# Sample rows in layer 1's paired products: the shared first product is made once and added twice, instead of being run into two accumulators

## What is computed

```python
def dil_layer(x, dil_fn, mem_kv, norm_g, w_in, q_norm_g, mem_q_g, w_out):
    z = rms_norm(x, norm_g) @ w_in                 # x: 2048 prompt rows, and 8 sample rows
    qd, gd, mq, mg = jnp.split(z, [...], axis=-1)
    ...
def shared_kv(x, kv_norm_g, w_kv, k_norm_g):
    kv = (rms_norm(x, kv_norm_g) @ w_kv)           # the same rows, another weight
    ...
```

## Time and profile before

| | |
|---|---|
| time, median of 3 runs | 2947.7 us (2941.38 to 2948.47) |
| span of the profiled execution | 2951.0 us |
| TensorE busy in it | 2819.4 us (96%) |
| VectorE busy | 1855.2 us (63%) |
| ScalarE busy | 1187.9 us (40%) |
| GpSimd busy | 461.8 us (16%) |
| mean DMA rate | 189 GB/s |

### The profile page before, as it was taken

One profiled execution on the slowest core, in us unless ns is written; L12 is line 12 of the kernel. 1 busy time (PEld: TensorE's weight loads), 2 busy tenths in 40 slices (PEclk: granted clock), 3 DMA queues, 4 the chain that ended last, 5 costly groups with the idle time before them and its releaser, 6 DMA issues. The chain is left out here.

```text
span 2951.0 us, 40709 instructions
## 1 busy us (share of the span) xinstructions
PE 2819.4 (96%) x13910; PEld 2315.7 (78%) x13910; DVE 1855.2 (63%) x3966; ACT 1187.9 (40%) x3494; POOL 461.8 (16%) x614
## 2 busy tenths in 40 slices
PE   7999999999998999979999999999999979989999
PEld 6787888888776888868778788777777768887787
DVE  4585766666785543334656667665746658877765
ACT  5432221312243242234343536323223458866642
POOL 0001010101000000000110202323331157640000
PEclk9999999999998999989999999999999989999999
DMA  4285645555675343232565667887776756646542
GB/s 170 84 251 192 191 154 185 183 171 178 219 243 169 108 150 107 72 133 101 192 241 194 238 203 249 258 276 223 262 250 222 266 194 210 199 145 226 198 145 98
DMA packets 281059, 556.96 MB, mean 189 GB/s; under 512 B 30385, under 2 KB 80113, under 8 KB 280873
## 3 DMA queue, kind: packets, MB, share of 16 engines
q1 hardware_dynamic: 248552, 455.99, 47.2%
q0 software_dynamic: 32320, 98.60, 9.7%
HBM read 421.76 MB, written 132.72 MB: 188 GB/s over the span
## 5 line engine op out<-in xcount | busy, mean ns | idle before, releaser
L109 PE MATMUL ps<-b_wp,b_sring 128*128 128x512 f32 x640 | 252.5, 395 | 17.8 <-DMA b_sring<-sums_dram 13.9
L110 PE MATMUL ps<-b_wp,b_sring 128*128 128x512 f32 x640 | 251.5, 393 | 0.0
L111 PE MATMUL ps<-b_wp,b_sring 128*128 128x512 f32 x640 | 251.5, 393 | 0.0
L109 PE MATMUL ps<-a_sring,a_wp 128*128 128x512 f32 x512 | 199.9, 390 | 2.2 <-DMA a_sring<-sums_a_dram 2.2
L111 PE MATMUL ps<-a_sring,a_wp 128*128 128x512 f32 x512 | 199.4, 389 | 0.0
L110 PE MATMUL ps<-a_sring,a_wp 128*128 128x512 f32 x512 | 199.4, 389 | 0.0
L908 DVE TENSOR_TENSOR shared_o<-ps,b_spare 128x512 f32<-128x512 f32 x160 | 109.8, 687 | 133.9 <-PE ps L111 114.9
L111 PE MATMUL ps<-b_wp,b_xtlo 128*128 128x512 f32 x496 | 193.2, 389 | 0.0
L109 PE MATMUL ps<-b_wp,b_xthi 128*128 128x512 f32 x480 | 186.9, 389 | 0.5 <-ACT b_spare L852 0.5
L110 PE MATMUL ps<-b_wp,b_xthi 128*128 128x512 f32 x480 | 186.8, 389 | 0.0
L669 POOL DMA_DIRECT2D kv_dram<-shared_o x102 | 56.3, 552 | 748.0 <-DVE shared_o L893 605.9
(11 more groups left out here) (492 smaller groups left out, 7528.9 us busy)
## 6 DMA issues: line engine op xcount, KB each, us to landing
b_sring<-sums_dram SPq DMA_DIRECT2D x160, 512.0 KB, 5.1
a_sring<-sums_a_dram SPq DMA_DIRECT2D x128, 512.0 KB, 5.0
b_raws<-w_b_dram SPq DMA_DIRECT2D x176, 256.0 KB, 4.0
a_raws<-w_a_dram SPq DMA_DIRECT2D x140, 256.0 KB, 4.3
kv_dram<-shared_o POOLq DMA_DIRECT2D x96, 256.0 KB, 4.0
tok_b_dram<-shared_o POOLq DMA_DIRECT2D x96, 256.0 KB, 4.7
front<-tok_b_dram SPq DMA_DIRECT2D x96, 256.0 KB, 3.2
front<-kv_dram SPq DMA_DIRECT2D x96, 256.0 KB, 4.1
```

The costliest lines, as they stand in the source:

```text
L109: pe.matmul(acc, a_hi, b_hi, start=first, stop=False)
L110: pe.matmul(acc, a_hi, b_lo, start=False, stop=False)
L111: return pe.matmul(acc, a_lo, b_hi, start=False, stop=last)
```

## The change

Pass 0's sample product is run once, into bank 4, and two steps earlier (ahead of product p = 5). ScalarE copies its partitions 32 to 39 to an SBUF row at step 6 (`zero_low`), and VectorE adds its partitions 0 to 7 and this row and writes the sum back to bank 4 (`zero_high`). Bank 5 then takes first pass 1's product alone, and later those of passes 5 and 6. `sample` on VectorE has one more add, of the sum that stands in bank 4. The row lies in the ring slot of the pair's first output tile, and that tile waits for `zero_high`. Four semaphores are new. Elsewhere `ps[:, 6:8, :]` gets the name `mem_banks`, left out here.

```diff
         if r == 2 * TP and j < len(pairs):
-            return sample_out(j, 0), 4, 2 * j
+            return sample_out(j, 0), 5, 2 * j
...
+    def zero_at(n):
+
+        j, r = divmod(n, PN)
+        return j if r == TP - 2 and j < len(pairs) else None
...
+        zero_sum = ps[0:S, 4, :]
+        zero_out = lambda j: CONV + j * 2 * SAMPLES
+        zero_row = lambda j: o[0:S, zero_out(j) % RING, :]
...
+            def zero_low(j):
+                act.wait_ge(zero_made, j + 1)
+                slot_free(zero_out(j))
+                act.activation(zero_row(j), ps[LOW:LOW + S, 4, :], ACT.Copy).then_inc(zero_copied, 1)
...
+                if zero_at(n) is not None:
+                    zero_low(zero_at(n))
                 if sample_at(n):
                     low_rows(*sample_at(n))
...
                     dve.wait_ge(acc_done, TP * j + p + 1)
+                    if p == 0:
+                        dve.wait_ge(zero_done, j + 1)
                     complete(out_of(n), product, acc(0, p))
...
+            def zero_high(j):
+                dve.wait_ge(zero_copied, j + 1)
+                if j:
+                    dve.wait_ge(zero_added, 2 * j)
+                dve.tensor_tensor(zero_sum, zero_sum, zero_row(j), ALU.add).then_inc(zero_done, 1)
...
                 dve.wait_ge(low_copied, 2 + n + 1)
                 at = o[0:S, i % RING, :]
+                dve.wait_ge(zero_done, n // 2 + 1)
+                dve.tensor_tensor(at, at, zero_sum, ALU.add).then_inc(zero_added, 1)
+                dve.wait_ge(zero_added, n + 1)
                 dve.tensor_tensor(at, ps[0:S, bank, :], at, ALU.add).then_inc(o_done if kinds[i] == "copy" else added, 1)
...
+                if zero_at(n) is not None:
+                    zero_high(zero_at(n))
                 if sample_at(n):
                     sample(*sample_at(n))
                 for at, u in key_unit.items():
...
                 if f == 0 and j:
                     pe.wait_ge(o_done, sample_out(j - 1, 1) + 1)
-                for bank in ((4, 5) if f == 0 else (4,) if f == 1 else (5,)):
-                    for k in range(HK):
-                        x = xs_hl[:, k + HK * (f in (1, 6)), :]
-                        acc = ps[0:LOW + S, bank, :]
-                        pe.matmul(acc, x, w[:, k, 0, :], start=(f == 0 and k == 0), stop=False)
-                        m = pe.matmul(acc, x, w[:, k, 1, :], start=False, stop=(f in (1, 6) and k == HK - 1))
+                if f == 5:
+                    pe.wait_ge(o_done, sample_out(j, 0) + 1)
+                acc = ps[0:LOW + S, 5 if f else 4, :]
+                for k in range(HK):
+                    x = xs_hl[:, k + HK * (f in (1, 6)), :]
+                    pe.matmul(acc, x, w[:, k, 0, :], start=(f != 6 and k == 0), stop=False)
+                    m = pe.matmul(acc, x, w[:, k, 1, :], start=False, stop=(f != 5 and k == HK - 1))
+                if f == 0:
+                    m.then_inc(zero_made, 1)
...
-                if p == TP - 1 and f in (0, 1, 5, 6):
+                if p == (TP - 1 if f else TP - 3) and f in (0, 1, 5, 6):
                     sample(j, f)
```

More of the change, by code:

```diff
@@ L528, in shared_stage @@
                  "m_squared m_rooted m_inverted m_scaled m_turned m_hi_done m_lo_done k_turned k_hi_done k_lo_done "
-                 "v_hi_done v_lo_done last_out")
+                 "v_hi_done v_lo_done zero_made zero_copied zero_done zero_added last_out")
         sems = core.sems(st, "shared", names)
@@ L535, in shared_stage @@
          wo_lo_done, m_squared, m_rooted, m_inverted, m_scaled, m_turned, m_hi_done, m_lo_done, k_turned, k_hi_done,
-         k_lo_done, v_hi_done, v_lo_done, last_out) = sems[28:]
+         k_lo_done, v_hi_done, v_lo_done, zero_made, zero_copied, zero_done, zero_added, last_out) = sems[28:]
         prep.open(st, lambda t: 4 + 2 * (t % 2))
@@ L545, in shared_stage @@
         tx_lo = tx.bitcast(F32R)
+        zero_sum = ps[0:S, 4, :]
+        zero_out = lambda j: CONV + j * 2 * SAMPLES
+        zero_row = lambda j: o[0:S, zero_out(j) % RING, :]
+        mem_banks = ps[:, 6:8, :]
         s_dram = io["sums"].rearrange("(n p) c -> n p c", p=P)
@@ L782, in mem_square @@
                 act.wait_ge(mem_in[m], 16)
-                act.activation(ps[:, 6:8, :].rearrange("p a b -> p (a b)"), mem[:, m, :], ACT.Square,
+                act.activation(mem_banks, mem[:, m, :].rearrange("p (a b) -> p a b", a=2), ACT.Square,
                                accum_out=mstat[:, m, 0:1]).then_inc(m_squared, 1)
@@ L792, in mem_high @@
                 act.activation(ops.mt_rows[0][:, :, :, m * P:(m + 1) * P],
-                               ps[:, 6:8, :].rearrange("p a (b t) -> p a b t", t=P), ACT.Copy).then_inc(m_hi_done, 1)
+                               mem_banks.rearrange("p a (b t) -> p a b t", t=P), ACT.Copy).then_inc(m_hi_done, 1)
             def keys_high(m):
@@ L1026, in mem_low @@
                 dve.wait_ge(m_hi_done, m + 1)
-                dve.tensor_tensor(ops.mt_rows[1][:, :, :, cols], ps[:, 6:8, :].rearrange("p a (b t) -> p a b t", t=P),
+                dve.tensor_tensor(ops.mt_rows[1][:, :, :, cols], mem_banks.rearrange("p a (b t) -> p a b t", t=P),
                                   ops.mt_rows[0][:, :, :, cols], ALU.subtract).then_inc(m_lo_done, 1)
@@ L1123, in turn_mem @@
                 for k in range(KD):
-                    t = pe.transpose(ps[:, 6 + k // 4, k % 4 * P:(k % 4 + 1) * P], mem[:, m, k * P:(k + 1) * P],
+                    t = pe.transpose(mem_banks[:, k // 4, k % 4 * P:(k % 4 + 1) * P], mem[:, m, k * P:(k + 1) * P],
                                      core.ident[:, :])
```

## The result

The changed kernel takes 2932.4 us (2928.6 to 2936.9 in nine runs), the kernel before, in nine runs taken with it, 2941.4 us: a ratio of 0.9970, with a 95% interval of 0.9960 to 0.9981. A second comparison on another occasion gave 0.9970 again (0.9958 to 0.9982). So the change makes the kernel faster by 0.30%, 9 us: as much as the 0.3% that the forecast took for the least that can be told. The forecast was -0.34% and 2937.8 us. The 5.4 us between the two times are no effect of the change: the three runs that the forecast started from had a median of 2947.7, and that of all nine is 2941.4, 6.3 us less.

A forecast was written before the change was run, and what follows sets the result against it. The pairs were taken to run at TensorE's pace, with a little lost in the last three. Removal 9.25 us plus move 0.73 us, added work and key reduce nothing, made 10.0 us less: 2937.8 us, range 2931.5 to 2946.

The forecast's parts named there:

- What is removed: TensorE, pass 0 of five pairs: 40 sample matmuls fewer at 0.231 us each, 9.25 us less.
- What is moved: Pair 1, pass 0: sample matmuls ahead of product 5 fill its wait for ScalarE's accumulator copy, 0.73 us less.
- What is added: One ScalarE copy (0.59 us) and three VectorE adds (0.68 us each) a pair: taken as nothing, at most 1 us.
- The key reduce: Pair 5, pass 0: reduce about 4.5 us late, GpSimd's next load 1.5 to 2 us late; cost taken as nothing.
- The sum: Whole kernel: 9.25 + 0.73 = 10.0 us less, -0.34%; chance of the forecast as worked out 0.60.
- Rival 1: Pairs 3 to 5: the ring's loads take the gain back, 4.4 us stay, 2943.3 us; chance 0.25, wholly or mostly.
- Rival 2: Pairs 3 to 5: ring and clock waits shrink too, some 5 us, 2933 us (or grow, 2943); downwards chance 0.09.
- Rival 3: Pairs 3 to 5: late key reduces delay GpSimd, VectorE and TensorE, 20 us in for 10 out, 2957 us; chance 0.06.
- The signs: Profile after: 160 sample matmuls, pairs 1 and 2 shorter by 2.6 and 1.85 us, no accumulator-copy wait in pair 1.
- The level: Whole kernel's time: the 10.0 us step put on the runs' median of 2947.7, giving 2937.8 us.

The follow-up runs named there:

- the kernel with the added work alone: The changed kernel with pass 0's sample product run twice into bank 4, so 16 matmuls again; ratio 0.9997 to the kernel before.
- the one with step 7: The changed kernel with pass 0's product made once but at its old place ahead of product 7; ratio 0.9981 to the kernel before.
- 16 matmuls at step 5: The kernel before with all 16 sample matmuls of pass 0 ahead of product 5 instead of 7; ratio 0.9999 to the kernel before.
- the kernel with eight adds: The changed kernel with the new add at each sample output made eight times instead of once; ratio 1.0044 to the kernel before.

## Why the prediction came out right, step by step

- **What is removed** (9.25 us): right, in place and size. Pair 2 fell from 161.7 to 159.9 us, 1.8 against 1.85 forecast, in every trace with eight. 24 matmuls more a pair cost 5.5 us, 0.23 us each, again. That it is the matmuls and nothing beside them is shown by the kernel with the added work alone, which has them back and takes 161.7 us again. The Trainium skill (TensorE: Matmul & The Clock Gate, Back-to-back issue gap) has about 131 ns for a matmul of 512 moving columns in a sustained stream. By that the forty would have been worth 5.2 us, an estimate; the runs don't bear it out.
- **What is moved** (0.73 us): right. The move alone took 0.8 to 1.0 us off pair 1, and without it the 0.5 us wait was back.
- **What is added** (nothing): right as to the sum, by the added work without the removal. The covers behind it were partly misjudged. Product 5 in pair 3 (3.2 us) was called the tightest place that was found. In the same trace products 7 and 8 of that pass had 1.6 and 1.4 us, and product 5 of pair 4 had 3.5, of which 0.2 were left in the changed kernel's second trace; with the removal and not the move TensorE waited 0.76 us there for VectorE's update. At the weights of pass 3 in pair 3, 0.3 us of cover were forecast to be left, and 0.2 were (last chunk ready at 1891.95, its first matmul at 1892.18). VectorE's idle time in a stretch, put at 50 to 60 us, is 54 to 66 by the rows, which changes nothing. So "nothing" is a sum in which waits below a microsecond are lost, and its margin was thin: seven adds more at each output made it 22 us. The prediction also priced a lost cover by its overshoot alone, where in pair 3 a late output tile and the lower clock behind the waits came on top.
- **The key reduce** (nothing): its delay came as forecast, and no cost of it can be shown.
- **The sum** (-10.0 us): measured -9 us, with an interval of 6 to 12. **Rival 1** (the ring's loads take it back in pairs 3 to 5) would have left 4.4 us, which lies outside the interval of both comparisons, and 24 matmuls more cost 15.3 us in pairs 3 to 5, nearly the full price. The traces of 8 and 16 alone would not settle it: pairs 3 to 5 were 506.2 to 514.6 us with 16 matmuls, mean 508.7, and 501.2 to 505.0 with 8 (five traces, the one with step 7 among them), mean 503.1. The difference of 5.6 us agrees with 3 x 1.85 = 5.55, but the four with 16 spread over more than that. **Rival 2** (the waits shrink by 5 us) describes the first two traces, but not the change: the ring's and the unnamed waits were 17.8 us in the first trace of before, 14.0 in the second and 12.1 with 16 matmuls at step 5, and 11.8 and 12.5 in the two of the changed kernel. **Rival 3** (slower through the key reduce) falls.
- **The signs**: the prediction called itself wrong if the waits in the last three pairs moved by more than 5 us. Between the first two traces they moved by 6.0 (17.8 to 11.8), and the unchanged kernel alone moved by 3.8. The sign was set too near to the scatter to tell anything. The others came as named: 160 sample matmuls, pairs 1 and 2 shorter by 2.6 and 1.8 us, no wait for the accumulator copy, and nobody on TensorE who waits for the new adds.
- **The level** (2937.8): 5.4 us too high, and only 0.9 us inside the lower end of the range (2931.5). The step that was off is the one that carried the three runs' median over: 2947.7 where nine runs give 2941.4. The forecast of the difference didn't depend on it; that the time still fell into the range was in part luck.

What stays open: how long each of the ring's waits is. It differs from execution to execution, and no run here separates the collisions of loads that make it.

## What to carry to other kernels

Where one engine is busy all through a stretch, a removed instruction is worth its start-to-start distance, and that can be read and forecast to the tenth of a microsecond; find such a stretch and judge the change by it, because the whole time and the stretches with waits scatter by more than the change is worth. A piece of work that may stand anywhere in a phase is best put just ahead of a place where the engine waits anyway; here that was worth 0.8 us in pair 1 as a by-product of the change, and about 2 us in pair 3 where it was done on purpose. Whether work on an engine that is mostly idle is free is read at each place where the busy engine needs its result, and not from the idle time of the stretch: one add took 0.7 us of cover where 6.8 us were there as where 3.2 were. Before a span of one trace is set against another, take a second trace of the same kernel: here the first pair of traces differed by 21 us, and the change was 9 of them.

## What was not expected of the hardware

Two executions of the same program differed by 12.2 us in span (2951.0 and 2938.8), and not only where TensorE waits: the part before the pairs took 1503.0 and 1500.7 us. VectorE's dependent adds of 8x512 in a row start 0.71 us apart (eight in 1891.39 - 1885.72 = 5.67 us), where the next instruction, which needs nothing of them, starts 0.61 us behind the last (1892.00 - 1891.39). So the dependence with its semaphore costs 0.10 us a step, though each row shows 0.67 to 0.69 us of duration. Behind two waits of TensorE of 2.0 and 3.1 us in the kernel with eight adds the granted clock was 0.63 in one stretch and 0.76 in the other, and while it was low matmuls started 0.43 us apart (1873.57, 1874.00, 1874.43) instead of 0.23, as at 1.2 GHz, the lower of the two levels.
